# Second RMS norm between out projection and FFN: its sum of squares put together from tile sums

## What is computed

```python
mix_out = merged @ w_out[l]
x = x + gate_m * rms_norm(mix_out, g_post_mix[l])
h2 = rms_norm(x, g_pre_ffn[l]) * (1 + scale_f) + shift_f
f = (jax.nn.silu(h2 @ w_ffn_gate[l]) * (h2 @ w_ffn_up[l])) @ w_ffn_down[l]
```

## Time and profile before

| | |
|---|---|
| median of 3 runs | 2366.13 us (2364.97 to 2366.26) |
| the profiled execution, its own time | 2366.21 us |
| its span in the trace | 2364.5 us |
| PE busy | 99% of the span |
| DVE busy | 70% |
| ACT busy | 47% |
| place of the change | about 640 to 675 us from the start |

### The profile page before, as it was taken

One profiled execution on the slowest core, in us unless ns is written; L12 is line 12 of the kernel. 1 busy time (PEld: TensorE's weight loads), 2 busy tenths in 40 slices (PEclk: granted clock), 3 DMA queues, 4 the chain that ended last, 5 costly groups with the idle time before them and its releaser, 6 DMA issues.

```text
span 2364.5 us, 31114 instructions
## 1 busy us (share of the span) xinstructions
PE 2349.5 (99%) x10779; PEld 1946.2 (82%) x10779; DVE 1646.0 (70%) x2048; ACT 1123.1 (47%) x1415; POOL 221.0 (9%) x450
## 2 busy tenths in 40 slices
PE   9999999999999999999999999999999999999998
PEld 7888788888888888888888888888888888888887
DVE  6998899999776666655544465665665567787664
ACT  4544546544464444444444455445644444444554
POOL 0001000000002112112100000000021132232000
PEclk9999999999999999999999999999999999999999
DMA  9986469999957877876666556665566675565454
GB/s 384 396 319 203 151 244 362 331 340 354 342 170 235 267 251 240 266 231 200 231 193 193 194 176 209 201 209 199 174 215 212 200 218 182 178 188 189 156 193 156
DMA packets 162325, 552.86 MB, mean 234 GB/s; under 512 B 23808, under 2 KB 25120, under 8 KB 161568
## 3 DMA queue, kind: packets, MB, share of 16 engines
q1 hardware_dynamic: 145584, 528.28, 66.1%
q0 software_dynamic: 13824, 14.18, 2.0%
q10 hardware_dynamic: 2800, 8.81, 1.0%
HBM read 534.91 MB, written 2.11 MB: 227 GB/s over the span
## 4 chain that ended last, share of the span: by engine, by line
PE 99%; DMA 0%; ACT 0%; DVE 0%; issue 0%; SPq 0%; ACTq 0%; DVEq 0%
PE acc L2090 30%; PE acc L2091 30%; PE acc L2097 30%; PE tb L2178 1%; PE tb L2619 1%; PE tb L2090 1%; PE tb L2091 1%; PE tb L2097 1%; PE acc L2146 0%; PE acc L2148 0%; PE acc L2147 0%; PE tb L2622 0%; PE tb L2365 0%; PE acc L2157 0%; DMA start_raw<-in_wa_dram 0%; PE tb L2206 0%
## 5 line engine op out<-in xcount | busy, mean ns | idle before, releaser
L1212 DVE TENSOR_TENSOR lo<-raw,hi 128x1024 fp32r<-128x1024 f32 x809 | 969.2, 1206 | 559.9 <-ACT hi L614 556.8
L614 ACT ACTIVATE hi<-raw 128x1024 fp32r<-128x1024 f32 x809 | 843.6, 1049 | 951.0 <-PE acc L2097 764.9
L2090 PE MATMUL acc<-hi,Hh 128*128 128x512 f32 x1960 | 774.4, 395 | 1.3 <-DVE Hl L1765 0.7
L2091 PE MATMUL acc<-hi,Hl 128*128 128x512 f32 x1960 | 763.9, 390 | 0.0
L2097 PE MATMUL acc<-lo,Hh 128*128 128x512 f32 x1960 | 524.5, 389 | 0.0
L2090 PEld LDWEIGHTS acc<-hi,Hh 128*128 128x128 f32 x1960 | 368.2, 188 | 78.9 <-issue 4.7
L2097 PEld LDWEIGHTS acc<-lo,Hh 128*128 128x128 f32 x1960 | 368.0, 188 | 77.2
L2091 PEld LDWEIGHTS acc<-hi,Hl 128*128 128x128 f32 x1960 | 368.3, 188 | 75.7 <-issue 1.4
L2090 PE MATMUL acc<-hi,hbh 128*128 128x512 f32 x512 | 204.1, 399 | 0.0
L2091 PE MATMUL acc<-hi,hbl 128*128 128x512 f32 x512 | 199.8, 390 | 0.0
L575 POOL DMA_DIRECT2D tok<-sgt x176 | 86.2, 498 | 851.0 <-DVE sgt L1338 811.3
(11 more groups left out here) (342 smaller groups left out, 2100.3 us busy)
## 6 DMA issues: line engine op xcount, KB each, us to landing
raw<-in_wa_dram SPq DMA_DIRECT2D x680, 512.0 KB, 4.4
late_raw<-in_wa_dram SPq DMA_DIRECT2D x96, 512.0 KB, 5.4
raw<-in_wb_dram SPq DMA_DIRECT2D x96, 512.0 KB, 4.3
start_raw<-in_wa_dram SPq DMA_DIRECT2D x64, 512.0 KB, 7.4
raw<-in_wc_dram SPq DMA_DIRECT2D x64, 512.0 KB, 4.2
tok<-sgt POOLq DMA_DIRECT2D x240, 32.0 KB, 4.6
landed<-sgt POOLq DMA_DIRECT2D x192, 32.0 KB, 4.0
x<-in_x_dram SPq DMA_DIRECT2D x2, 1024.0 KB, 6.2
```

The costliest lines, as they stand in the source:

```text
L614: act.activation(hi[:, s, 0:n], raw[:, r, 0:n], ACT.Copy).then_inc(hi_ready, 1)
L1212: dve.tensor_tensor(lo[:, s, 0:n], raw[:, r, 0:n], hi[:, s, 0:n].bitcast(F32), ALU.subtract)\
L2090: pe.matmul(dst(tt), a, hi[:, s, w], start=first and i == 0, stop=False)
L2091: pe.matmul(dst(tt), b, hi[:, s, w], start=False, stop=False)
```

## The change

The sum of squares of the new x is no longer taken from x. With r the reciprocal root of the first norm, the new x is x + r mix, so the mean of its squares is mean(x x) + r (2 mean(x mix) + r mean(mix mix)). The three means are gathered by tile. mean(x x) is kept from the first norm of the program (`x_mean`). ACT squares each tile of `mix` (`square_mix`). DVE multiplies `mix` with x with an accumulated sum (`cross_sum`). When r is there, four DVE instructions on one column each (`cross`, `quad`, `poly` twice) put the sum together and ACT takes the root (`sum_root`). `square_sum` and `sum_x` on ACT and DVE go. The eight updates of x stay but are spread: `add_x(tt, i)` stands between the other steps, the last one of half 1 behind the first FFN unit's split. `keep_warm` does 20 products in place of 27. The transfer of x into SBUF is issued where it was, but DVE now waits for it before the splits of units OUT0+29 to OUT0+31.

```diff
@@ ScalarE
+            def square_mix(i, tt):
+
+                act.wait_ge(mix_ready, TT * i + tt + 1)
+                act.activation(junk[:, tt, :], mix[:, tt, chunk(i)], ACT.Square, scale=D ** -0.5, accum_out=mixsq[:, tt, i:i + 1])\
+                    .then_inc(mix_squared, 1)
             for t in range(3):
                 split_to(OUT0 + 8 * t + 11)
                 square_tile(t % 2, t)
...
+                split_to(OUT0 + 8 * t + 13)
+                for tt in range(TT):
+                    square_mix(t, tt)
...
-            def square_sum(tt):
-                for i in range(4):
-                    act.wait_ge(x2_ready, c.up("x2"))
-                    act.activation(junk_x[:, tt, chunk(i)], x[:, tt, chunk(i)], ACT.Square, accum_out=ssqp[:, tt, i:i + 1])\
-                        .then_inc(half_squared, 1)
+            def sum_root(tt):
+                act.wait_ge(poly_ready, tt + 1)
+                act.activation(std[:, tt:tt + 1], poly[:, tt:tt + 1], ACT.Sqrt, bias=x_mean[:, tt:tt + 1]).then_inc(half_std, 1)
...
             square_out(0)
+            square_mix(3, 0)
+            sum_root(0)
             split(1)
-            square_sum(0)
             finished(FFN0 - 1)
             square_out(1)
-            half_root(0, base + 2)
-            split(1)
-            square_sum(1)
-            half_root(1, base + 3)
-            split(1)
+            square_mix(3, 1)
+            sum_root(1)
+            split(2)
@@ VectorE
+            def cross_sum(i, tt):
+                dve.wait_ge(mix_ready, TT * i + tt + 1)
+                if i > 0:
+                    dve.wait_ge(crossed, TT * (i - 1) + tt + 1)
+                dve.scalar_tensor_tensor(sgt[:, tt, :], mix[:, tt, chunk(i)], 2.0 / D, x[:, tt, chunk(i)], ALU.mult, ALU.mult,
+                                         accum_out=xmix[:, tt, i:i + 1]).then_inc(crossed, 1)
+
+            split_to(OUT0 + 29)
+            dve.wait_ge(x_loaded, 16)
+            for i in range(3):
+                for tt in range(TT):
+                    cross_sum(i, tt)
+                split(1)
...
+            def normed(tt):
                 dve.wait_ge(half_squared, c.up("squared"))
+                dve.tensor_tensor(mix[:, tt, chunk(3)], acc[:, 2 + tt, :], gm1[:, chunk(3)], ALU.mult).then_inc(mix_ready, 1)
+                cross_sum(3, tt)
+                dve.sem_inc(acc_free[2 + tt], 1)
                 half_inverse(rstd, tt)
+                add_x(tt, 0)
+                dve.wait_ge(crossed, TT * 3 + tt + 1)
+                dve.tensor_reduce(cross[:, tt:tt + 1], xmix[:, tt, :], AX_X, ALU.add)
+                dve.wait_ge(mix_squared, TT * 3 + tt + 1)
+                chain(dve.tensor_reduce(quad[:, tt:tt + 1], mixsq[:, tt, :], AX_X, ALU.add))
+                chain(dve.scalar_tensor_tensor(poly[:, tt:tt + 1], quad[:, tt:tt + 1], rstd[:, tt:tt + 1], cross[:, tt:tt + 1], ALU.mult, ALU.add))
+                dve.tensor_scalar(poly[:, tt:tt + 1], poly[:, tt:tt + 1], rstd[:, tt:tt + 1], floor[:, tt:tt + 1], ALU.mult, ALU.max)\
+                    .then_inc(poly_ready, 1)
+                add_x(tt, 1)
                 half_inverse(rstd2, tt)
                 for i in range(2):
                     dve.tensor_scalar(mix[:, tt, chunk(i)], x[:, tt, chunk(i)], rstd2[:, tt:tt + 1], None, ALU.mult)\
                         .then_inc(xn_ready, 1)
+                add_x(tt, 2)
...
-            add_out(0)
+            normed(0)
+            add_x(0, 3)
             split(1)
-            sum_x(0)
-            add_out(1)
-            scale_x(0)
-            sum_x(1)
-            scale_x(1)
+            normed(1)
...
             split_x(0).then_inc(tb_free[0], 1)
             dve.sem_inc(tb_free[1], 1)
             split(1)
+            add_x(1, 3)
@@ TensorE
-            keep_warm(0, 27, mergedh, mergedl)
+            keep_warm(0, 20, mergedh, mergedl)
```

More of the change, by code:

```diff
@@ L243, in two_blocks @@
         best8 = sb("best8", [P, TT, 8])
+        x_mean = sb("x_mean", [P, TT])
+        floor = sb("floor", [P, TT])
+        mixsq = sb("mixsq", [P, TT, 4])
+        xmix = sb("xmix", [P, TT, 4])
+        quad = sb("quad", [P, TT])
+        cross = sb("cross", [P, TT])
+        poly = sb("poly", [P, TT])
         sgt = sb("sgt", [P, TT, N])
@@ L374, in two_blocks @@
         queries_taken = sem("queries_taken")
+        mix_ready = sem("mix_ready")
+        mix_squared = sem("mix_squared")
+        poly_ready = sem("poly_ready")
+        crossed = sem("crossed")
         hid_blocks = sem("hid_blocks")
@@ L892, in _ @@
             split_to(FFN0)
-            base = c.up("base", 3) - 3
+            base = c.up("base")
             def square_out(tt):
@@ L898, in square_out @@
                 c.up("squared")
[L899 to L907 removed]
+                half_root(tt, base)
+            def sum_root(tt):
+                act.wait_ge(poly_ready, tt + 1)
+                act.activation(std[:, tt:tt + 1], poly[:, tt:tt + 1], ACT.Sqrt, bias=x_mean[:, tt:tt + 1]).then_inc(half_std, 1)
             act.wait_ge(half_done, c.up("half"))
             square_out(0)
+            square_mix(3, 0)
+            sum_root(0)
             split(1)
[L912 removed]
             finished(FFN0 - 1)
             square_out(1)
[L915 to L919 removed]
+            square_mix(3, 1)
+            sum_root(1)
+            split(2)
             def scaled_hi(kt, b, at):
@@ L931, in scale_x @@
             def scale_x(i):
+                act.wait_ge(x2_ready, 4 + i + 1)
                 for tt in range(TT):
@@ L1517, in _ @@
             split_to(V3)
+            dve.tensor_copy(x_mean[:], var[:])
+            chain(dve.tensor_scalar(floor[:], var[:], -1.0, EPS, ALU.mult, ALU.add))
             dve.wait_ge(ssq_ready, c.up("ssq"))
@@ L1700, in _, with gated_tile @@
                 merge_b(j)
-            def gated_tile(dst, gains, pair, col):
+            def gated_tile(dst, gains, pair, col, done=None):
                 dve.wait_ge(gate_loaded, 16 if gains is gm1 else 32)
@@ L1706, in gated_tile @@
                     dve.wait_ge(evac, c.up("evac"))
-                    dve.tensor_tensor(dst[:, tt, cols(col, N)], acc[:, 2 * pair + tt, :], gains[:, cols(col, N)], ALU.mult)\
-                        .then_inc(acc_free[2 * pair + tt], 1)
+                    ins = dve.tensor_tensor(dst[:, tt, cols(col, N)], acc[:, 2 * pair + tt, :], gains[:, cols(col, N)], ALU.mult)
+                    ins.then_inc(acc_free[2 * pair + tt], 1)
+                    if done is not None:
+                        dve.wait_ge(acc_free[2 * pair + tt], TILES_BEFORE_OUT // 2 + col // N // 2 + 2)
+                        dve.sem_inc(done, 1)
             def add_normed(src):
@@ L1721, in _ @@
                 split_to(OUT0 + 8 * t + 11)
-                gated_tile(mix, gm1, t % 2, t * N)
-            split_to(FFN0)
+                gated_tile(mix, gm1, t % 2, t * N, mix_ready)
+            def cross_sum(i, tt):
[10 more added lines that the diff above has]
+                split(1)
             add_bias(SCALE_F, 2 * KD)
@@ L1726, in _, with add_x @@
             base_of(slice(0, TT))
-            dve.wait_ge(x_loaded, 16)
-            c.up("half")
-            def add_out(tt):
+            def add_x(tt, i):
+                dve.scalar_tensor_tensor(x[:, tt, chunk(i)], mix[:, tt, chunk(i)], rstd[:, tt:tt + 1], x[:, tt, chunk(i)],
+                                         ALU.mult, ALU.add).then_inc(x2_ready, 1)
+            def normed(tt):
                 dve.wait_ge(half_squared, c.up("squared"))
-                dve.tensor_tensor(mix[:, tt, 3 * N:], acc[:, 2 + tt, :], gm1[:, 3 * N:], ALU.mult).then_inc(acc_free[2 + tt], 1)
+                dve.tensor_tensor(mix[:, tt, chunk(3)], acc[:, 2 + tt, :], gm1[:, chunk(3)], ALU.mult).then_inc(mix_ready, 1)
+                cross_sum(3, tt)
+                dve.sem_inc(acc_free[2 + tt], 1)
                 half_inverse(rstd, tt)
[L1735 to L1740, removed]
+                add_x(tt, 0)
[7 more added lines that the diff above has]
+                add_x(tt, 1)
                 half_inverse(rstd2, tt)
@@ L1745, in scale_x @@
                         .then_inc(xn_ready, 1)
-            def sum_x(tt):
-                dve.wait_ge(half_squared, c.up("squared", 4) - 1)
-                base_of(slice(tt, tt + 1))
-            add_out(0)
+                add_x(tt, 2)
+            c.up("half")
+            normed(0)
+            add_x(0, 3)
             split(1)
-            sum_x(0)
-            add_out(1)
-            scale_x(0)
-            sum_x(1)
-            scale_x(1)
+            normed(1)
             def scaled(kt, b, at, k):
```

## The result

The changed kernel takes 2420.93 us, median of 4 runs (2420.2 to 2421.43), against 2366.14 for the kernel before on the same chip: a ratio of 1.0234 [1.0222, 1.0246], 54.8 us slower. The forecast was 2366.6, within 2364.6 to 2369.6: the kernel lost a hundred times the 0.5 us that was forecast.

The account below looks back on a forecast made before the run. PE, busy 99% of the span, bounds the kernel, with DVE the chain at the norms: 0 there, +0.3 to the first FFN unit, +0.2 at the second, +0.5 on 2366.21, forecast 2366.6 us, range 2364.6 to 2369.6.

Parts of the forecast that it names:

- Behind it: After the norms' transposes: first FFN unit +0.3 us, second shifted 0.5 in all, then the FFN as before.
- Half 0: DVE's work on the first token half at the norms: 7.06 us, so half 1 starts 1.7 later.
- half 1: DVE's work on the second token half up to its normed chunk at the norms: 3.79 us.
- accumulator read: DVE's reading of the sum in `cross_sum` at the norms: 0.10 us taken, bounds 0 and 0.20.
- the four small instructions that make `poly`: DVE's one-column instructions in each half at the norms: 0.60 us together, bounds 0.10 or 0.20 each.
- the +0.2 charged to the second unit: At the second FFN unit: a later `Hl`, plus 0.94 us until PE starts, adds 0.2 to the first unit's +0.3.
- The lower bound of the sum: Least total change at the norms, from accumulator reads (-0.2) and small instructions (-0.4): put at +0.0 us.
- the rival with a chance of 0.25: PE's clock falls behind its 2.3 us gap at the norms: total +0.5 +0.8 to +3.4 us, middle 2368.7; chance 0.25.
- `cross_sum` at half the rate: Rival: each `cross_sum` on DVE takes 0.53 us more, total 2369.3 or more; chance 0.07.
- The chain does get shorter: Rival at the norms: transposes at 667.1, FFN unit 1.3 to 1.6 us earlier, total 2364.9; chance 0.08.

Follow-up runs that it names:

- b_shift224: The kernel before with 224 unused bytes ahead of `sgt` and all tiles behind it, no instruction changed: 2421.05 us, ratio 1.0232.
- a_same: The changed kernel with its small tiles packed so that all large tiles stand where they stood in the kernel before: 2365.97 us, ratio 1.0002.
- a_packed: The changed kernel with five of the small tiles in one, so the rest moves 128 bytes in place of 224: 2414.18 us, ratio 1.0205.
- a_early: On a_same: DVE's last update of half 0 and the split behind it moved after half 1, one ACT copy to `hi` earlier: 2364.04 us, ratio 0.9994.

## Why the prediction was wrong

**The step that failed** is the last one of "Behind it": that behind the second unit "nothing more is lost and the FFN runs as before". Every duration was taken over from the trace of before, PE's 3.19 for a unit with them, though the new tiles put the operands of each product at another distance. The prediction costed instructions, waits and queues, and put the seven allocation lines of the new tiles at nothing without a word, neither as a cost nor as a rival (the diff under "The change" doesn't show them either). In their place the runs showed 6.2 ns more for each product with `hi` or `lo`. Those seven lines cost 55 us and the rest nothing that can be told from the spread. That it is they was shown from both sides: b_shift224 has only the move and loses 55 us (2421.05), a_same has all but the move and loses none that can be told (2365.97).

The size fits the count. The trace of before has 7090 products with `hi` or `lo` behind 675 us; at 6.2 ns each they lose 44 us, and 44 are seen. From 120 us to the norms it has 2124, and there the difference is only 5.0 ns (0.2281 before, 0.2331 after), since some of before's products are slow already, between 240 and 300 us with 0.2301 on average. That makes 10.7 us. At 107 us the changed kernel is 0.9 late (the same split of DVE stands at 106.76 and 107.63), together 11.6, and 11.4 are seen. What slows before's own products there was not looked into.

**The steps at the norms, read in a_same.** Half 0 took 7.00 (7.06 forecast), half 1 3.74 (3.79). Within this `cross_sum` stepped by 0.62 and its accumulator read is hidden, where 0.77 was forecast; the four small instructions that make `poly` took 0.69 (660.78 to 661.47), where 0.60 was forecast. Two errors nearly cancelled. The transposes stand 6.81 behind the idle products' start, before 6.91: nothing gained, as forecast. The first FFN unit is 9.93 behind it (before 9.82) and the second 13.16 (before 13.01): +0.15 at most, where +0.5 was forecast. Of the +0.2 charged to the second unit 0.04 showed: PE began it 0.75 behind its `Hl` (675.51 to 676.26), where 0.94 had been taken over from the first unit. The lower bound of the sum was off as well: +0.5 less 0.2 and 0.4 is -0.1, not 0.0. The medians' +0.55 has an interval of about 2 us either way and can't choose between the two, so that it meets the forecast's +0.5 is no proof of the sum.

**The gap and the clock.** PE stood still for 1.94 in the changed kernel and 2.12 in a_same (2.3 forecast). The clock did fall in the profiled run of the changed kernel. Two stretches of it, one of a_packed, where PE had stood still for 1.95, and two of a_same:

```profile
679.90:683.30 3.40, 3.40 (x15) 0.50 0.00 0
684.00:690.00 6.00, 6.00 (x32) 1.00 0.45 154
```

```profile
678.00:681.40 3.40, 3.40 (x11) 0.50 0.00 0
```

```profile
37.80:44.40 6.60, 6.60 (x30) 0.50 1.02 404
670.00:673.00 3.00, 2.10 (x15) 1.00 0.00 0
```

In the changed kernel it was at 1.2 GHz for 3.4 us, behind the 1.94 of standing still (the first four transposes last 1.05 in place of 0.63), and back at 2.4 when the first unit began: its first product, at 683.56, steps by 0.23. In a_same, after 2.12, the stretch of 670 to 673 shows 1.00. So the rival with a chance of 0.25 came true in two of the three profiled executions with such a gap, and the ground for holding it unlikely, that the clock had stood 2.4 us at the end of the program, was no ground: it fell behind shorter gaps. From the transposes to the first unit it is 3.68 in the one and 3.12 in the other: 0.56, less than the least that I had given it (0.8). 0.22 of it lie between the normed chunk and the first `Hl`, which needs the transposed blocks (2.98 and 2.76), and 0.34 between that `Hl` and the unit (1.29 and 0.95). In the changed kernel this last part isn't a wait for `Hl`: the three idle products behind the transposes, slow as well, last until the unit begins. The 11 runs of a_same spread from 2365.22 to 2368.2, and four of them lie over 2366.9 (one of the 27 of before does); that a falling clock at the norms makes these was not shown. The profiled one, at 2367.6, speaks against it: it had 1.00 there, and of the 1.4 that it is over before's 2366.21 it had 1.28 already when the idle products began (663.10 against 661.82). Its own low stretch lay at 38 to 44 us.

**The other rivals.** `cross_sum` at half the rate is out: 669.26 to 669.88 is 0.62 for 512 columns, no more than a product (0.61). The Trainium skill, "Vector Engine (DVE) Microarchitecture Reference", section "Points that are easy to get wrong", has this kind of instruction at half throughput. If that is half of a product's rate, as the prediction took it, this trace doesn't agree. "The chain does get shorter" was false for this order of work and true for a_early's: the new form of the sum takes 3.75 for half 1 where it was 5.40, and the order of the change gave these 1.6 us back ahead of half 1, where one update and one split could have waited.

**The distance.** What was measured is this: distances that differ from before's by 0, 256 or 512 bytes leave the time at 2365.3 to 2365.4; by 32, 64 or 224 make it 2420.6 to 2421.3; by 128 make it 2414.2. Before's own are multiples of 1024 where I worked them out (`hi` to `Hh` 67 x 1024, to `hidh` 99 x 1024). All are for float32 operands of 128x128 against 128x512, and these seven values are the only ones tried, each for `hi` and `lo` alike. A reading as "multiples of 256 are free" fits them all, with 256 itself tried once; what in the memory or in PE's reading of it makes it so stays open, and other types and shapes weren't tried.

## What to carry to other kernels

A diff's allocation lines are part of its cost. Ask of each new tile what it moves, and in a kernel in which one engine is busy for 99% multiply every change of its step by the count: some 6 ns, over 9,500 products, was 55 us. If a change slows instructions that it doesn't touch, run the kernel before with its tiles moved alike before looking anywhere else; one such kernel decided here what no reading of the norms could. Put small tiles behind the large ones, or see that the large ones stay as far from each other as they were: packing alone (a_packed) gave back only 7 of the 55 us. And where a sum gathered early shortens a chain, see that the order spends the gain on the chain and not on work that could wait.

## What the runs showed of the hardware

- In this kernel's float32 products a step depends on where moving and stationary operand lie to each other in a partition: 0.227 us at the distances tried that are multiples of 256 bytes (0.227 for the idle products as well), 0.233 at remainders 32, 64 and 224, a little less at 128 (2414.3 us in all against 2421). The listed mean of a product with `Hl` moves only from 390 to 395 ns. Moving everything together by 64 changes nothing, and the difference is there with ACT, DVE and POOL at rest. The Trainium skill, "TensorE: Matmul & The Clock Gate", section "Step-by-step: what each phase is for", says that loading the next weights takes no SBUF bandwidth from the running product; by that alone the place of the two would not matter, and the runs show that it does.
- Reading DVE's accumulator is listed at 0.08 us and costs no step; on ACT it was listed at 0.194.
- PE's clock was at 1.2 GHz for 3.4 us behind 1.94 us without work in one execution and behind 1.95 in another, and it held behind 2.12 in a third; in the earlier trace rows it was still at 2.4 GHz after 2.4 us without work.
